# Up projections of three MLP quarters computed in the orientation of the down projections, a quarter of their products Strassen-like, with the results turned back by TensorE

## The chip, the cores and the metric

The kernel runs on one core of one Trainium2 chip. The metric is the device time of one execution in microseconds (us); for the kernel before it is 1199.64 us, the median of 3 runs (1199.57 to 1199.95).

## What is computed

One layer of a decoder over 256 tokens with 2048 channels: three kinds of attention and an output projection, a cross attention, and an MLP. The change touches the MLP alone:

```python
def rms_norm(x, g):
    y = x32 * lax.rsqrt(jnp.mean(x32 * x32, axis=-1, keepdims=True) + RMS_EPS)
    return (y * g.astype(jnp.float32)).astype(x.dtype)
...
h = rms_norm(x, g_mlp[l])
x = x + jnp.einsum('bsf,fd->bsd', jnp.square(jax.nn.relu(jnp.einsum('bsd,df->bsf', h, w_up[l]))), w_down[l])
```

`w_up` is 2048 x 8192 and `w_down` is 8192 x 2048, both float32.

## The kernel before

**Numbers.** Each float32 operand is split in a high part, rounded to the type fp32r, and a low part, the remainder. A product is three matmuls: high times high, high times low, low times high. ScalarE (ACT) makes the high half of a weight tile from `staged` into `w_high` (128x1024), VectorE (DVE) subtracts and writes `w_low`, and TensorE (PE) takes both. `w_high` and `w_low` hold four such halves; ACT may write half h when PE is done with half h-4 (semaphore `half_done`), DVE follows it (`high_ready`), PE follows DVE (`low_ready`). Weights come by DMAs of 1 MB on SyncE's queue into four slots of `staged`.

**The MLP.** The 8192 hidden channels are four quarters of 16 tiles of 128. For each quarter the up projection comes first, then the down projection.

- *Up* (L1539, `job_of` L1310, `half_job` L1282): one job for each of the 16 hidden tiles. The weight block is stationary, the 256 tokens are moving: for two blocks of the depth (`kt` even and odd) there are a 512-column matmul of the high weight with both parts of the tokens, two 256-column matmuls of the low weight, and another 512-column one. A job has 8 such pairs. Its output is laid channels by tokens; ACT and DVE make relu, the norm's factor (a row of `factor` by tokens), the square and the split, and put the tile into `part_b`.
- *Down* (`down_group` L1581): a quarter's outputs stay by tokens, 1024 channels in each of two groups. Here the activations are stationary (128 tokens), the weights moving with 512 columns. A quarter of the depth (the first unit of 4 blocks) is computed by seven products in place of eight, Strassen's scheme in the Winograd form: `s_half` (L1563) is one product, 6 matmuls, with sums of weight blocks that DVE makes in place (`sum_of_weights`, L1139) and sums of tokens (`sums_of_tokens`, L1102). The other three units are ordinary: four `r_half` (L1543) each, 12 matmuls in one. So a group has 7 x 6 + 12 x 12 = 186 matmuls of 512 columns. Halves in a group are numbered: 0 to 2 are three products, 3 to 6 the first ordinary unit, 7 to 10 the four products with sums (11 is counted together with 10), 12 to 19 the last two units. DVE adds the seven products and the four PSUM sums into `y` in 12 steps (`step`, L1158; semaphore `y_step`). The last four steps of a group stand in DVE's queue among the first halves of the group that follows.
- The fourth quarter's up and down projections are ordinary; between its up jobs PE turns `y` by two 128x128 transposes a job (L1632), so that DVE can add it to `x`.

**The start of the MLP.** The cross attention's output projection (`short_jobs`, JOB_CO) runs while ACT and DVE (`grow`, L625 and L1018) add its results to `x`, scale and split them into `part_a`, and split the first MLP weights. PE's first up job waits for `x2_low`, `low_ready` and `taken`. GpSimd (POOL) sums squares for the norm, which PE ends with `norm_sum` (L1352), and clears `y` (L411).

What sets the order of the work is each engine's queue, written out by hand, with the semaphores; nothing is scheduled by a tool.

## Time and profile before

| | |
|---|---|
| median of 3 runs | 1199.64 us (1199.57 to 1199.95) |
| the profiled execution, its own time | 1199.49 us |
| its span, first to last instruction | 1197.7 us |
| PE busy | 1181.8 us, 99% of the span |
| DVE busy | 853.0 us, 71% |
| ACT busy | 628.7 us, 52% |
| mean granted TensorE clock | 0.998 |

The profile's page gives, for one execution, how long each engine was busy; the trace behind it gives the start and the length of each instruction. A matmul is shown longer than it takes from PE's time, since matmuls overlap: the distance from one start to the next is what one costs. Times in the rows are us from the span's start, if not marked ns.

### The profile page before, as it was taken

Reading aid. Unit: us, or ns where it says so; the run is one execution under the profiler, and the core shown is the slowest. Engines: PE = TensorE matmul, PEld = TensorE weight load, DVE = VectorE, ACT = ScalarE, POOL = GpSimd, SP = SyncE. Lnnn points to the kernel's source line nnn. Section 1 sums busy time; section 2 is a strip of 40 time slices with the busy share of each in tenths; the row PEclk is TensorE's granted clock in tenths of the full one; section 3 lists DMA queues with packets and bytes.
Section 4 is the critical chain, followed back from the end, with each engine's and each line's share of the span. In section 5 each row is a group of like instructions: output and inputs, shape, how many; then the busy total and the mean of one; then the engine's idle time right before and its main releaser. Section 6 shows DMA issues by size and latency. Waiting matters only on the chain.

```text
span 1197.7 us, 19269 instructions
## 1 busy us (share of the span) xinstructions
PE 1181.8 (99%) x6776; PEld 1035.5 (86%) x6776; DVE 853.0 (71%) x1149; ACT 628.7 (52%) x927; POOL 177.6 (15%) x177
## 2 busy tenths in 40 slices
PE   9999999999999999999999999999999999999996
PEld 7888899999989989888888888888888888888885
DVE  5758766786667967676887666877767787666554
ACT  6445455554645657565544555544656454555442
POOL 2907400030322504300000000000000000000341
PEclk9999999999999999999999999999999999999999
DMA  9664543443644543455456454647454746555541
GB/s 361 251 256 170 205 176 140 149 167 140 231 161 171 186 166 141 145 207 202 175 178 252 176 178 172 211 150 271 175 177 140 274 156 221 189 177 187 199 140 70
DMA packets 51455, 224.43 MB, mean 187 GB/s; under 512 B 3792, under 2 KB 4176, under 8 KB 31696
## 3 DMA queue, kind: packets, MB, share of 16 engines
q1 hardware_dynamic: 50688, 220.22, 51.3%
q10 hardware_dynamic: 720, 3.59, 0.8%
q8 instruction: 30, 0.49, 0.2%
q14 instruction: 17, 0.14, 0.0%
HBM read 221.69 MB, written 2.10 MB: 187 GB/s over the span
## 4 chain that ended last, share of the span: by engine, by line
PE 94%; DVE 3%; ACT 1%; issue 1%; POOL 1%; DMA 1%; SPq 0%; DVEq 0%; ACTq 0%; POOLq 0%
PE bank L1303 16%; PE bank L1300 16%; PE bank L1301 15%; PE extra L1557 6%; PE extra L1559 5%; PE extra L1558 5%; PE bank L1305 4%; PE bank L1307 4%; PE bank L1306 4%; PE bank L1346 3%; PE bank L1348 3%; PE bank L1347 3%; DVE w_low L813 1%; PE bank L1570 1%; PE bank L1572 1%; PE bank L1571 1%
## 5 line engine op out<-in xcount | busy, mean ns | idle before, releaser
L813 DVE TENSOR_TENSOR w_low<-staged,w_high 128x1024 fp32r<-128x1024 f32 x311 | 390.1, 1269 | 145.3 <-ACT w_high L433 133.8
L433 ACT ACTIVATE w_high<-staged 128x1024 fp32r<-128x1024 f32 x304 | 314.5, 1053 | 188.9 <-PE bank L1303 80.4
L1301 PEld LDWEIGHTS bank<-part_a,w_low 128*128 128x128 f32 x1408 | 264.6, 188 | 61.3
L1300 PE MATMUL bank<-part_a,w_high 128*128 128x512 f32 x704 | 281.0, 399 | 1.2 <-DVE w_low L813 1.2
L1303 PE MATMUL bank<-part_a,w_high 128*128 128x512 f32 x704 | 278.5, 396 | 0.0
L1301 PE MATMUL bank<-part_a,w_low 128*128 128x256 f32 x1408 | 276.8, 278 | 0.0
L719 ACT ACTIVATE w_high<-staged 128x1024 fp32r<-128x1024 f32 x114 | 119.1, 1059 | 107.8 <-PE extra L1559 85.6
L1133 DVE TENSOR_TENSOR w_low<-staged,w_high 128x1024 fp32r<-128x1024 f32 x114 | 137.4, 1221 | 32.4 <-ACT w_high L719 31.0
L361 POOL TENSOR_TENSOR squares<-x 128x256 f32<-128x256 f32 (+1 forms) x31 | 36.2, 1168 | 681.8 <-DVE x L1257 658.2
L1300 PEld LDWEIGHTS bank<-part_a,w_high 128*128 128x128 f32 x704 | 133.7, 190 | 2.0 <-DVE w_low L813 1.2
L1303 PEld LDWEIGHTS bank<-part_a,w_high 128*128 128x128 f32 x704 | 131.9, 187 | 0.0
L1557 PE MATMUL extra<-w_high,part_b 128*128 128x512 f32 x288 | 112.7, 391 | 0.2
L1559 PE MATMUL extra<-w_high,part_b 128*128 128x512 f32 x288 | 112.1, 389 | 0.0
L1558 PE MATMUL extra<-w_low,part_b 128*128 128x512 f32 x288 | 112.1, 389 | 0.0
L1305 PE MATMUL bank<-part_a,w_high 128*128 128x256 f32 x384 | 110.1, 287 | 0.1
L1307 PE MATMUL bank<-part_a,w_low 128*128 128x256 f32 x384 | 108.7, 283 | 0.0
L1306 PE MATMUL bank<-part_a,w_high 128*128 128x256 f32 x384 | 108.6, 283 | 0.0
L1098 DVE TENSOR_TENSOR part_b<-hidden,part_b 128x256 f32 (+1 forms) x64 | 27.2, 426 | 71.6 <-ACT part_b L701 71.6
L1305 PEld LDWEIGHTS bank<-part_a,w_high 128*128 128x128 f32 x384 | 73.7, 192 | 0.5 <-POOL part_a L375 0.4
L1306 PEld LDWEIGHTS bank<-part_a,w_high 128*128 128x128 f32 x384 | 73.6, 192 | 0.1
L1307 PEld LDWEIGHTS bank<-part_a,w_low 128*128 128x128 f32 x384 | 73.6, 192 | 0.0
L699 ACT ACTIVATE hidden<-spare 128x256 f32<-128x256 f32 x64 | 26.7, 418 | 76.8 <-DVE spare L1094 76.8
(201 smaller groups left out, 1803.2 us busy)
## 6 DMA issues: line engine op xcount, KB each, us to landing
staged<-in_wup SPq DMA_DIRECT2D x64, 1024.0 KB, 4.8
staged<-in_wdown SPq DMA_DIRECT2D x64, 1024.0 KB, 5.1
staged<-in_wqk SPq DMA_DIRECT2D x32, 1024.0 KB, 4.8
staged<-in_wv SPq DMA_DIRECT2D x12, 1024.0 KB, 4.9
staged<-in_wbc SPq DMA_DIRECT2D x8, 1024.0 KB, 4.8
staged<-in_wmk SPq DMA_DIRECT2D x4, 1024.0 KB, 4.7
staged<-in_woa SPq DMA_DIRECT2D x4, 1024.0 KB, 4.7
staged<-in_wcq SPq DMA_DIRECT2D x4, 1024.0 KB, 4.9
```

The source lines that it names most:

```text
L433: nc.scalar.activation(w_high[:, job % 2, cols], staged[:, job % 4, cols], ACT.Copy).then_inc(high_ready, 1)
L813: tt(w_low[:, job % 2, cols], staged[:, job % 4, cols], f32(w_high[:, job % 2, cols]), ALU.subtract).then_inc(low_ready, 1)
L1133: tt(half_4d(w_low, h), src, f32(half_4d(w_high, h)), ALU.subtract).then_inc(low_ready, made)
L1300: mm(out[:, :], high, both, start=first, stop=False)
L1301: last = mm(out[:, 0:T], low, part[:, slot(kt), 0, :], start=False, stop=False)
L1303: last = mm(out[:, :], high, both, start=False, stop=last_tile)
L1305: mm(out[:, 0:T], high, part[:, slot(kt), 0, :], start=first, stop=False)
L1306: mm(out[:, 0:T], high, part[:, slot(kt), 1, :], start=False, stop=False)
L1307: last = mm(out[:, 0:T], low, part[:, slot(kt), 0, :], start=False, stop=last_tile)
L1557: mm(out[:, :], part_b[:, kt, 0, tokens], high, start=opens, stop=False)
L1558: mm(out[:, :], part_b[:, kt, 0, tokens], low, start=False, stop=False)
L1559: last = mm(out[:, :], part_b[:, kt, 1, tokens], high, start=False, stop=ends)
```

## The change

The three quarters whose down projection was by groups have their up projection by the same kind of groups. A quarter is now four groups of 20 halves, 0 and 1 up, 2 and 3 down, each 186 matmuls of 512 columns with the activations stationary (`part_a` for up, `part_b` for down). The weights are loaded by the same DMAs as in the down groups. What comes with it:

- The sums of tokens of the MLP's input (`part_x`) are made once, at the start, from four tiles that ACT scales again (`x2_gained`).
- An up group's sums are by tokens (`common`, four 128x512 pieces), gathered by 8 DVE steps (`up_step`). In the group that follows ACT makes relu with the norm's factor as a scale by partition (`relu`, 2 x 128x1024), squares it (`relu_square`, 2 x 128x1024), and PE turns it by 16 transposes of 128x128, in two batches of 8 (`hidden_turn`), into PSUM banks 2 and 3; ACT (`hidden_high`) and DVE (`hidden_lows`) split each batch into `part_b`. The first batch of group 1 is also copied to `quad`, from which DVE makes the sums of tokens.
- The first group of all has an order of its own (`PLACES`): its third product comes after the first ordinary unit.
- The products that used bank 3 use bank 0.
- `up` by jobs is left for the fourth quarter.

```diff
 SUMMED_QUARTERS = 3
 GROUP_HALVES = 20
-GROUP_STEPS = 12
-QUARTER_HALVES = 2 * QUARTER + 2 * GROUP_HALVES
+UP_STEPS, DOWN_STEPS = 8, 12
+QUARTER_STEPS = 2 * UP_STEPS + 2 * DOWN_STEPS
+QUARTER_HALVES = 4 * GROUP_HALVES
...
+PLACES = {False: (2, (3, 4, 5, 6)), True: (6, (2, 3, 4, 5))}
...
+            def relu(q, group, t):
+
+                act.wait_ge(y_step, group_steps(q, group) - 1 + t)
+                nc.scalar.activation(by_token[:, t, :], common[:, 2 * t:2 * t + 2, :].rearrange("p a c -> p (a c)"),
+                                     ACT.Relu, scale=factor[:, F_X2, T + t:T + t + 1]).then_inc(relu_made, 1)
+
+            def relu_square(q, group, t):
+                act.wait_ge(relu_made, turned_before(q, group) + t + 1)
+                nc.scalar.activation(by_token[:, t, :], by_token[:, t, :], ACT.Square).then_inc(square_made, 1)
+
+            def hidden_high(q, group, n):
+                tile = 8 * (group - 1) + 4 * n
+                act.wait_ge(group_turned, turned_before(q, group) + n + 1)
+                if tile == 0:
+                    nc.scalar.activation(quad[:, :, :], hidden_turned, ACT.Copy).then_inc(turned_moved, 1)
+                nc.scalar.activation(part_b[:, tile:tile + 4, 0, :], hidden_turned, ACT.Copy).then_inc(turned_high, 1)
...
+            def mlp_group(q, group, ahead=None):
+                turns = group in (1, 2)
+                if turns:
+                    relu(q, group, 0)
+                r_first(q, group, 1)
+                if turns:
+                    relu(q, group, 1)
+                r_first(q, group, 2)
+                if turns:
+                    for t in range(QT):
+                        relu_square(q, group, t)
+                move_common(q, group)
+                r_first(q, group, 3)
+                if turns:
+                    hidden_high(q, group, 0)
+                rest_of_group(q, group)
+                for n in range(4):
+                    (next_group if ahead is None else ahead)(q, group + 1, n)
...
+            grow(JOB_CO, OUT_CO, part_a, lambda t: t, G_MLP, x2_high, x2_low, first_ahead)
+            dve.wait_ge(taken, BANKS + OUT_MLP)
+            dve.sem_inc(y_step, FREE_STEPS)
+            dve.wait_ge(x2_scaled, 4)
+            sums_of_tokens(x2_gained, 0)
+            r_first(0, 0, 2, True)
+            sum_of_weights(0, 0, 0)
+            sums_low(part_x, x2s_high, 1, x2s_low)
+            r_first(0, 0, 3, True)
...
+            def hidden_turn(q, group, n):
+
+                for j in range(4):
+                    for t in range(QT):
+                        last = nc.tensor.transpose(hidden_turned[:, j, t * P:(t + 1) * P],
+                                                   by_token[:, t, (4 * n + j) * P:(4 * n + j + 1) * P], ident)
+                last.then_inc(group_turned, 1)
...
+                for n in range(4):
+                    r_half(q, group, 3 + n, n, 1, (0, 1))
+                    if turns and n == 1:
+                        pe.wait_ge(square_made, turned + 2)
+                        pe.wait_ge(turned_low, turned)
+                        hidden_turn(q, group, 0)
+                products(q, group, turns)
...
+            pe.wait_ge(y_step, FREE_STEPS - 4)
+            pe.wait_ge(x2_low, 4)
+            s_half(0, 0, 0, bank[0], block_of(0, 0, 0), ends=True)
+            s_half(0, 0, 1, extra[0], block_of(0, 1, 0))
...
+            norm_sum(N_X2, bank[3], cols=True)
```

Two places of the order. First PE, where the MLP starts: the last rows of the cross projection and the first of the MLP, before:

```order
L1306 MATMUL bank<-part_b,w_high 128x256
L1307 MATMUL bank<-part_b,w_low 128x256
L1300 MATMUL bank<-part_a,w_high 128x512 [waits x2_low,low_ready,taken]
L1301 MATMUL bank<-part_a,w_low 128x256 x2
L1303 MATMUL bank<-part_a,w_high 128x512
```

and with the change:

```order
L1410 MATMUL banks<-part_b,w_high 128x256
L1411 MATMUL banks<-part_b,w_low 128x256
L1671 MATMUL banks<-w_high,part_a 128x512 [waits low_ready,x2_low,y_step]
L1672 MATMUL banks<-w_low,part_a 128x512
L1673 MATMUL banks<-w_high,part_a 128x512
```

The first MLP matmul waits for `y_step` in place of `taken`. DVE counts `y_step` up after all its work of `grow`, which is the second place: DVE's queue at the end of `grow`, before:

```order
L1031 TENSOR_TENSOR x<-x,bank 128x256
L1023 SCALAR_TENSOR_TENSOR part_a<-x,gains,part_a 128x256 [waits x2_high] x4
L813 TENSOR_TENSOR w_low<-staged,w_high 128x1024 [waits high_ready]
L1230 UNCONDITIONAL_BRANCH [waits y_clear,factor_ready,taken]
L1230 ISA
L813 TENSOR_TENSOR w_low<-staged,w_high 128x1024 [waits high_ready]
```

and with the change:

```order
L1106 TENSOR_TENSOR x<-x,banks 128x256
L1098 SCALAR_TENSOR_TENSOR part_a<-x,gains,part_a 128x256 [waits x2_high] x4
L1205 TENSOR_TENSOR w_low<-staged,w_high 128x1024 [waits high_ready]
L1190 TENSOR_TENSOR token_sums<-by_token 128x2x128 [waits taken,x2_scaled]
L1191 TENSOR_TENSOR token_sums<-by_token 128x2x128
L1193 TENSOR_TENSOR token_sums<-token_sums,by_token 128x2x128 [waits token_made]
L1195 TENSOR_TENSOR token_sums<-by_token,token_sums 128x2x128 [waits token_made]
L1205 TENSOR_TENSOR w_low<-staged,w_high 128x1024 [waits high_ready]
L1219 TENSOR_TENSOR staged<-staged 128x2x4x128
L1199 TENSOR_TENSOR part_x<-token_sums,part_x 128x2x512 [waits x2s_high]
```

The counting up itself (a semaphore instruction) stands behind the third row there; the sums of the input's tokens and the first sum of weights come where the first up job's work stood.

Third, ACT in a group with turns (here group 1), from its second weight half of the first ordinary unit on, with the change:

```order
L766 ACTIVATE by_token<-common,factor 128x1024 [waits y_step]
L735 ISA
L731 REGISTER_ALU [waits landed1]
L732 ACTIVATE w_high<-staged 128x1024 [waits half_done]
L770 ISA
L771 ACTIVATE by_token<-by_token 128x1024 [waits relu_made]
L770 REGISTER_ALU
L771 ACTIVATE by_token<-by_token 128x1024 [waits relu_made]
L760 REGISTER_ALU [waits half_done]
L761 ACTIVATE common<-banks 128x512 [waits y_step]
L731 REGISTER_ALU
L732 ACTIVATE w_high<-staged 128x1024 [waits half_done]
```

ACT does relu, the next weight half and both squares ahead of the copy of `common` and the last weight half of the unit; before, nothing but the copy stood between weight halves there.

## Rows read from the trace of the kernel before

**Rows 1.** The page's first part: busy time, share of the span, instructions.
```profile
PE 1181.8 (99%) x6776; PEld 1035.5 (86%) x6776; DVE 853.0 (71%) x1149; ACT 628.7 (52%) x927; POOL 177.6 (15%) x177
```

**Rows 2.** Waits of PE from 450 us on: total us, times, longest.
```profile
PE bank L1300 <- DVE w_low L813: 1.2, 2, 0.9
```

**Rows 3.** Stretches: length, busy us (instructions) of PE, PEld, DVE, ACT, POOL; PEclk, DMA.
```profile
480.13:571.48 91.35, 90.19 (x516) 78.21 (x515) 62.65 (x95) 51.66 (x86) 8.27 (x6) 1.00 0.51 183
571.48:613.99 42.51, 42.48 (x188) 34.81 (x186) 34.71 (x37) 21.26 (x23) 0.00 (x0) 1.00 0.56 198
613.99:656.24 42.25, 42.25 (x187) 34.81 (x186) 34.65 (x35) 20.55 (x20) 0.00 (x0) 1.00 0.59 210
656.24:745.41 89.17, 89.17 (x514) 77.81 (x512) 60.59 (x89) 50.19 (x79) 0.00 (x0) 1.00 0.51 183
...
919.47:1004.35 84.88, 84.78 (x374) 69.56 (x372) 69.36 (x72) 41.82 (x43) 0.00 (x0) 1.00 0.57 202
```

**Rows 4.** PE in order of time, around transposes: start, length, line, operation.
```profile
427.85 0.60 PE L1510 MATMUL extra<-square,values 128*128 128x128 f32 x4
428.21 0.48 PE L1346 MATMUL bank<-w_high,part_b 128*128 128x512 f32 x1
428.52 0.39 PE L1347 MATMUL bank<-w_low,part_b 128*128 128x512 f32 x1
...
1009.91 0.38 PE L1632 MATMUL extra<-square,values 128*128 128x128 f32 x2
1010.05 0.48 PE L1300 MATMUL bank<-part_a,w_high 128*128 128x512 f32 x1
```

**Rows 5.** The stretch of the fourth quarter's 16 up jobs with their 32 transposes.
```profile
1004.35:1097.13 92.78, 92.78 (x546) 80.96 (x545) 63.19 (x94) 48.91 (x77) 0.00 (x0) 1.00 0.50 178
```

**Rows 6.** PE and DVE in order of time where the MLP starts.
```profile
480.13 0.40 PE L1300 MATMUL bank<-part_a,w_high 128*128 128x512 f32 x1
...
480.33 1.75 DVE L813 TENSOR_TENSOR w_low<-staged,w_high 128x1024 fp32r<-128x1024 f32 x1
...
482.68 1.66 DVE L1023 SCALAR_TENSOR_TENSOR part_a<-x,gains,part_a 128x256 fp32r<-128x256 f32 x4
484.35 1.23 DVE L813 TENSOR_TENSOR w_low<-staged,w_high 128x1024 fp32r<-128x1024 f32 x1
```

**Rows 7.** ACT and POOL there, in order of time.
```profile
484.22 0.71 ACT L646 ACTIVATE squares<-x 128x256 f32<-128x256 f32 x2
...
486.92 3.52 POOL L411 MEMSET values<- 128x4096 f32 x1
```

**Rows 8.** DVE and ACT in order of time at the start of the group of 613.99.
```profile
614.28 1.41 DVE L1176 TENSOR_TENSOR values<-values,extra 128x512 f32<-128x512 f32 x2 [0.49 <-PE extra L1559]
615.60 1.22 DVE L1148 TENSOR_TENSOR staged<-staged 128x1024 f32<-128x1024 f32 x1
616.74 1.22 DVE L1133 TENSOR_TENSOR w_low<-staged,w_high 128x1024 fp32r<-128x1024 f32 x1
...
614.19 1.06 ACT L719 ACTIVATE w_high<-staged 128x1024 fp32r<-128x1024 f32 x1 [1.66 <-PE extra L1559]
...
634.67 2.01 ACT L719 ACTIVATE w_high<-staged 128x1024 fp32r<-128x1024 f32 x2 [0.31 <-PE extra L1572]
```

**Rows 9.** PE at that group's half 3, in order of time.
```profile
618.07 0.46 PE L1557 MATMUL extra<-w_high,part_b 128*128 128x512 f32 x1
```

**Rows 10.** An ACT group by line from 460 us on: count, busy us, mean ns, idle before.
```profile
L699 ACT ACTIVATE hidden<-spare 128x256 f32<-128x256 f32 x64 | 26.7, 418 | 76.8 <-DVE spare L1094 76.8
```

**Rows 11.** The clock: PE's last row, and stretches as in rows 3.
```profile
1187.87 0.70 PE L1650 MATMUL extra<-squares,square 128*128 128x256 f32 x2 [0.99 <-ACT squares L798]
...
1192.60:1193.60 1.00, 0.00 (x0) 0.00 (x0) 1.00 (x2) 0.00 (x0) 0.00 (x0) 0.51 0.72 291
...
1.11:4.68 3.57, 3.57 (x8) 2.86 (x9) 0.00 (x0) 1.38 (x2) 0.23 (x1) 1.00 0.74 170
4.68:6.46 1.78, 1.78 (x9) 1.38 (x7) 0.61 (x2) 0.84 (x3) 0.00 (x0) 1.00 1.01 314
```

More of the change, by code:

```diff
@@ L307, in _, with load_unit @@
             stream(wco_in, JOB_CO, CROSS)
-            def load_up(q):
-                with sp.Fori(0, QUARTER // 4) as i:
-                    for s in range(4):
-                        load(wup_in[q * 16 + i * 4 + s, :, :], mlp(q, i), JOB_MLP + s)
-            def load_unit(q, g, unit, slot, free):
+            def load_unit(src, q, group, unit, slot, free):
                 for n in range(2):
@@ L623, in _, with grow, next_half @@
                     outputs_a(1)
-            def grow(job, n_out, norm, part, slot, gain, ready, free):
+            def grow(job, n_out, norm, part, slot, gain, ready, free, ahead=None):
+                def next_half(s, half):
+                    if ahead is not None and s >= 2:
+                        ahead(2 * (s - 2) + half)
+                    else:
+                        split(none, job + s + 2, half)
                 for s in range(4):
@@ L640, in grow @@
                         if late:
-                            split(none, job + s + 2, half)
+                            next_half(s, half)
                         for t in tiles:
@@ new lines, in first_ahead, with last_ahead @@
+            def first_ahead(n):
+                if n < 2:
+                    s_tile(0, 0, n, n)
+                else:
+                    r_first(0, 0, n - 2, True)
+            def last_ahead(q, group, n):
+                split(mlp(3), JOB_MLP + n // 2, n % 2)
+            grow(JOB_CO, OUT_CO, N_X2, part_a, lambda t: t, G_MLP, x2_high, 1, first_ahead)
+            for t in range(4):
+                nc.scalar.activation(x2_gained[:, t, :], x[:, t, :], ACT.Copy,
+                                     scale=gains[:, G_MLP + t:G_MLP + t + 1]).then_inc(x2_scaled, 1)
@@ L1035, in grow @@
                             lows((t, t + 1))
-                        split(none, job + s + 2, half)
+                        if ahead is not None and s >= 2:
+                            ahead(2 * (s - 2) + half)
+                        else:
+                            split(none, job + s + 2, half)
             dve.wait_ge(taken, BANKS + OUT_OA)
@@ new lines, in sums_of_tokens @@
+            def sums_of_tokens(src, made):
+                blocks = src.rearrange("p (a k) (m n) -> p a k m n", a=2, m=2)
+                first, second = ([blocks[:, :, k, m, :] for k in range(2)] for m in range(2))
+                to = [token_sums[:, :, n, :] for n in range(4)]
+                tt(to[0], second[0], second[1], ALU.add).then_inc(token_made, 1)
+                tt(to[2], first[0], second[0], ALU.subtract).then_inc(token_made, 1)
+                dve.wait_ge(token_made, made + 1)
+                tt(to[1], to[0], first[0], ALU.subtract).then_inc(token_made, 1)
+                dve.wait_ge(token_made, made + 3)
+                tt(to[3], first[1], to[1], ALU.subtract).then_inc(token_made, 1)
@@ new lines, in up_step @@
+            def up_step(q, group, n):
+                c11, c12, c21, c22 = (common[:, k, :] for k in range(4))
+                to, one, two = ((c12, c11, bank[2]), (c21, c12, bank[0]), (c22, c21, bank[1]), (c12, c12, bank[1]),
+                                (c11, c11, extra[0][:, :]), (c21, c21, extra[2][:, :]),
+                                (c12, c12, extra[1][:, :]), (c22, c22, extra[3][:, :]))[n]
+                wait_for_step(q, group, n, {0: H_SUMS + 3, 4: H_C + 2, 6: H_C + 4})
+                tt(to, one, two, ALU.add).then_inc(y_step, 1)
@@ new lines, in _ @@
+            right_below(0, 0, PLACES[True][0], False)
+            products(0, 0, False)
+            pe.wait_ge(x2_low, KT)
+            for n in range(4):
+                r_half(0, 0, H_B + n, n, 2, ())
+            norm_sum(N_X2, bank[3], cols=True)
+            for n in range(4):
+                r_half(0, 0, H_C + n, n, 3, ())
+            with pe.Fori(0, SUMMED_QUARTERS - 1) as q:
+                for group in range(1, 5):
+                    mlp_group(q, group)
+            for group in range(1, 4):
+                mlp_group(SUMMED_QUARTERS - 1, group)
```

552 lines of the change are left out of this document (283 added, 269 removed).

## The prediction, made before the changed kernel ran

> **What bounds the kernel.** First the page's engine shares: PE is busy for 99% of the span, DVE for 71%, ACT for 52% [rows 1]. A busy PE proves little, since matmuls are shown overlapping, so next PE's waits: over the whole MLP two waits of 1.2 us in all, both in the first up jobs [rows 2]. Then the stages: an up quarter is 89.17 us, a quarter's two down groups 84.88, the later group of the first pair 42.25 [rows 3]. In all of them PE goes from matmul to matmul. So the time of the MLP is PE's columns and instructions, plus any hand-off that now comes late. The sum goes over the stretch from 480.13 (first up matmul) to 1004.35 (first up matmul of the fourth quarter); what follows is the same code in both kernels, and what comes before is too. In the kernel before, this stretch is 524.22 us.
>
> **Term 1, the up quarters become groups.** Out go 91.35 us and twice 89.17. In come six groups of 186 matmuls. A down group is the same instructions with another stationary operand, so it is priced by 42.25: 42.25 / 186 = 0.2272 us a matmul. All twelve groups make 507.0 us. Taken against the groups that were there (42.51 + 42.25 + 2 x 84.88 = 254.5), the new six cost 252.5 and replace 269.7. I take 42.25, not 42.51, because the 0.26 more of the first group comes from DVE, which arrives there from an up quarter with work left over; in the new kernel every group but one follows a group.
>
> **Term 2, the transposes.** 2 batches of 8 for each of 2 up groups a quarter: 96 in all. Four transposes take 427.85 to 428.21, and the matmul behind them takes 0.31 where 0.23 is normal [rows 4]: 0.44, or 0.11 each. The fourth quarter has 32 between its jobs and is 92.78 - 89.17 = 3.61 us longer [rows 3, 5], 0.113 each. A batch of 8: 0.88 to 0.90; twelve of them: **10.7 us**. The low end is the pace inside a pair, 0.14 us from its start to the next matmul [rows 4], or 0.07 each with 0.08 once for a batch: 0.64, in all 7.7.
>
> **Term 3, the start.** PE is done with the cross projection at 480.13 and went straight on. Now its first matmul also waits for `y_step`, which DVE counts up only behind the last split of `grow`. DVE's queue there is a split of 1.75 from 480.33, two additions, four low parts from 482.68, and another split from 484.35 [rows 6]. No row shows whether a semaphore instruction goes while the operation before it runs. I take it that it does, since it needs nothing of the split, and PE starts at about 484.5; the late end is the split's own, 485.6. The new gap is **4.4 us** (to 5.5). In exchange what the old first quarter had over a plain one goes (91.35 is taken out whole, 2.2 above 89.17: two waits of 1.2 in all [rows 2] and the norm's sum). The new first group then has room: ACT ends its squares at 484.93 [rows 7] and makes four scaled tiles by 486.7; DVE needs 1.5 us for four additions, then split (1.14), sum, low sums, split. Half 4 is ready at 489.4 and wanted at 484.5 + 2 x 1.36 + 2 x 2.73 = 492.7; half 5 at 492.8, wanted 495.4; half 7, four more DVE passes later, at 498.5, wanted 499.5. Nothing late. The norm's sum with its two new column matmuls: **0.7**, an estimate, since 2.2 less 1.2 leaves 1.0 for the sum and the restarts of PE after its waits.
> At this place row and rule can be weighed. A DVE pass with both inputs in SBUF took 1.75 and not 1.23 while POOL was adding [rows 6]; POOL's clearing of `y` (3.52 us from 486.92 [rows 7]) ran while DVE had nothing to do, so no row tells whether it holds DVE. If it did, the first group's chain would come 3.7 us later and the sum grow by 2.8. The Trainium skill, page "SBUF — State Buffer", section "SBUF: two separate sides", says that a DVE operation with two SBUF inputs contends only with a GpSimd operation that reads SBUF; a clearing reads nothing, and by that rule the sum stays.
>
> **Term 4, inside a group with turns** (times from its first matmul). PE reaches the turn at 18 + 24 matmuls = 9.5. ACT: half 3 ends at 1.26 [rows 8]; relu, half 4, relu, half 5 and two squares, six passes at 0.96, the second of two back to back (2.01 less 1.06 [rows 8]), end at 7.0; the copy of `common` and half 6 at 8.5. PE does not wait. The turn ends at 10.4. In group 1 ACT now copies twice (to 12.7), DVE subtracts (14.0, a 128x1024 pass from PSUM taken as 1.14, the distance in rows 8; as two 128x512 steps it would be 1.41 [rows 8]), makes half 7 (15.1; wanted 15.9), half 8 (16.3), the four sums of tokens (17.8) and half 9 (19.0, seen by PE 19.15). Half 9 is wanted at 15.9 + 2.73 = 18.6: late by 0.54, three times: **1.6 us**. In group 2 a copy and the sums are missing, so nothing is late. The second batch comes between ordinary halves of 2.73 us each; the low parts are ready 1.5 to 2 us before the last unit wants them. The extra DVE and ACT work of an up group is hidden by its 42.25 us (a down group leaves DVE 7.6 and ACT 21.7 us free [rows 3], and an up group has 8 steps where down has 12).
> At each group's edge the chain is tight already: DVE's two last steps, a sum of weights and half 3 start at 614.28, 615.60 and 616.74 [rows 8] and PE takes half 3 at 618.07, its first matmul there shown 0.46 long [rows 9]. It has no slack and no loss. An up group's last steps are of the same shape, so I add nothing. DMAs: the same 1 MB loads, asked for at the same halves as in a down group, where PE waited for none.
>
> **Sum.** 4.4 + 507.0 + 10.7 + 1.6 + 0.7 = 524.4 against 524.2: +0.2 us. The profiled execution took 1199.49 with a span of 1197.7, so I predict 1199.7; the median of the runs, 1199.64, lies 0.15 above that execution, and I leave this aside. A measurement of this kernel can tell a change of about 0.2%, 2.4 us: below 1197.2 is faster, above 1202.0 slower.
>
> **The rivals.**
> *The clock falls in the gap.* PE stood for 4.06 us after its last matmul and then the granted clock was 0.51, the level of 1.2 GHz [rows 11]; the new gap is 4.4 us. At the program's start eight matmuls took 3.57 us where nine later took 1.78 [rows 11]: about 1.8 us lost before the clock is back. 1201.5. For it: the gap's length; against: the fall is seen once, after a sparse stretch. The Trainium skill, page "TensorE: Matmul & The Clock Gate", Part 1, has idle stretches throw PE back to 1.2 GHz and calls the moment run-variable; the trace agrees with the fall.
> *Each group costs what the first did*, 42.51: DVE's tight edge slips because the up groups add a little to its chain. 12 x 0.26 = 3.1: 1202.8.
> *ACT's chain comes late* (the slower side): relu, squares and copies run at four times the 256-wide rate, 0.418 [rows 10], 1.67 a pass. The point is 1.55 us: four passes, two halves at 0.96 and 1.26 must end by 9.4. At 1.67 the turn waits 0.5 us, six times, and group 1's two copies bring half 9 later by 1.4, three times: +7.2, 1206.9. Against: one 128x1024 pass took 1.06 [rows 8].
> *Clearing `y` blocks DVE*: 1202.5, as above.
> *The transposes run at the pair's inner pace*: -3.0, 1196.7. Against: both longer rows say 0.11.
> *The change does not do what it says*: the seven products save 6 of 192 matmuls a group, 1.36 us; that much is counted in the instructions, and only the up stage's price could differ with `part_a` stationary. The rows give no sign of it.
>
> **How the numbers follow.** My sum: 0.50, with most of it within 0.2%. Clock: 0.12, its price just below the bound, a half of it slower. Group edge 0.12, ACT late 0.08, clearing 0.05, all slower. Transposes cheaper 0.13, faster. Of my sum I give 0.02 to faster and 0.03 to slower for hand-offs mis-sized. Faster 0.15, same 0.51, slower 0.34. The range leaves out ACT's case and the tails: 1196.5, just under the cheap transposes, to 1204.0, which takes in the late end of the start (+1.1) with any one of the three other slower rivals.
>
> **What would show it.** Right: PE's first MLP matmul near 484.5, groups of 42.25 us, those with two turns 44.0, group 1 about 44.6, transposes x8 with 0.9 to the next matmul's end, and the fourth quarter starting near 1004.5. Wrong: PE waits on ACT's `by_token` (ACT late), a PEclk under 1.00 near 485 (clock), or a group period off by more than 0.2 us.

## The result: slower by 0.25%, and the profile after

| | before | after |
|---|---|---|
| median, 13 runs each on one chip | 1199.56 us (1199.27 to 1200.30) | 1202.44 us (1201.54 to 1204.56) |
| the profiled execution, its own time | 1199.49 us | 1202.02 us |
| its span | 1197.7 us | 1200.2 us |
| mean granted clock | 0.998 | 0.995 |

The ratio is 1.0025, with a 95% interval of 1.0016 to 1.0033: slower, by a little more than what the prediction called measurable. The time lies inside the predicted range, 2.7 us above the predicted 1199.7; by the prediction's own bound of 1202.0 it is slower, which had 0.34, and not the same, which had 0.51. The first part of the page, which answers to [rows 1]:

```profile
PE 1181.2 (98%) x6456; PEld 1022.5 (85%) x6456; DVE 888.3 (74%) x1097; ACT 639.6 (53%) x848; POOL 177.3 (15%) x177
```

PE has 320 instructions fewer and is busy 0.6 us less, while the span is 2.5 us longer. So look at where PE stood. PE's waits from 450 to 1010 us (total, times, longest) answer to [rows 2]; the second row lies in the cross attention, ahead of the MLP, and before has such a wait of 0.8 us too:

```profile
PE banks L1671 <- DVEq L1335: 4.2, 1, 4.2
PE banks L1636 <- DVE qk L1151: 0.8, 1, 0.8
```

One wait in the MLP, at its first matmul, on DVE's sequencer: on the counting up of `y_step`. Then the stages, to be held against [rows 3, 5]: columns as there. The first row is the gap, the second the first group; then groups 1, 2 (with turns), 3, 4 (without), 5, 6 (with), 7; last the fourth quarter's up jobs.

```profile
480.86:485.17 4.31, 0.16 (x3) 0.00 (x1) 4.30 (x9) 2.39 (x5) 2.40 (x3) 1.00 0.00 0
485.17:530.09 44.92, 44.92 (x193) 36.92 (x194) 33.71 (x34) 23.30 (x28) 5.90 (x4) 0.96 0.53 187
530.09:574.40 44.31, 44.27 (x204) 36.46 (x202) 36.72 (x38) 27.74 (x28) 0.00 (x0) 1.00 0.54 190
574.40:618.50 44.10, 44.10 (x204) 36.47 (x202) 36.83 (x37) 25.77 (x26) 0.00 (x0) 1.00 0.56 191
618.50:660.74 42.24, 42.24 (x188) 34.82 (x186) 34.66 (x35) 20.43 (x20) 0.00 (x0) 1.00 0.58 199
660.74:703.00 42.26, 42.26 (x188) 34.65 (x186) 32.07 (x31) 20.44 (x20) 0.00 (x0) 1.00 0.58 200
703.00:747.49 44.49, 44.45 (x204) 36.59 (x204) 36.72 (x38) 27.75 (x28) 0.00 (x0) 1.00 0.55 190
...
1006.85:1099.63 92.78, 92.78 (x546) 81.00 (x545) 62.92 (x94) 48.91 (x77) 0.00 (x0) 1.00 0.50 177
```

Groups without turns take 42.24 and 42.26, as the down groups did before, groups with turns 44.05 to 44.49, and the fourth quarter's 92.78 is the 92.78 of [rows 5]. What doesn't fit is in the first two rows: PEclk 0.96 in the first group, and a start at 480.86 where before it was 480.13. PE in order of time at the MLP's start (start, length, line, operation, idle before and its releaser), against [rows 6]:

```profile
485.17 0.50 PE L1671 MATMUL banks<-w_high,part_a 128*128 128x512 f32 x1 [4.15 <-DVEq L1335]
485.50 0.40 PE L1672 MATMUL banks<-w_low,part_a 128*128 128x512 f32 x1
...
486.24 0.63 PE L1672 MATMUL banks<-w_low,part_a 128*128 128x512 f32 x1
486.66 0.63 PE L1673 MATMUL banks<-w_high,part_a 128*128 128x512 f32 x1
...
489.61 0.39 PE L1659 MATMUL extra<-w_high,part_a 128*128 128x512 f32 x1
```

and the stretch in which the granted clock was at 1.2 GHz, by its row:

```profile
486.15:489.56 3.41, 3.41 (x9) 2.65 (x9) 2.39 (x6) 2.58 (x5) 3.33 (x3) 0.50 0.00 0
```

After the gap of 4.31 us PE ran for 1.0 us at full speed, then eight matmuls stood 0.43 us apart in place of 0.23. The twelve matmuls of the first two products took 489.61 - 485.17 = 4.44 us. The clock fell, as the first rival had it (e1 will show what they take without the fall). DVE and POOL at the same place:

```profile
485.08 1.23 DVE L1205 TENSOR_TENSOR w_low<-staged,w_high 128x1024 fp32r<-128x1024 f32 x1
487.29 0.70 DVE L1190 TENSOR_TENSOR token_sums<-by_token 128x256 f32<-128x256 f32 x1 [0.98 <-ACT by_token L836]
487.91 0.41 DVE L1191 TENSOR_TENSOR token_sums<-by_token 128x256 f32<-128x256 f32 x1
...
489.04 1.22 DVE L1205 TENSOR_TENSOR w_low<-staged,w_high 128x1024 fp32r<-128x1024 f32 x1
```
```profile
485.50 2.21 POOL L388 TENSOR_TENSOR acc<-acc,quad 128x256 f32<-128x256 f32 x2 [2.08 <-ACT quad L670]
487.65 3.52 POOL L429 MEMSET values<- 128x4096 f32 x1
```

DVE's split starts at 485.08. The counting up of `y_step` stands behind it in DVE's queue, and still PE starts at 485.17: the semaphore went while the split ran, not at its end. And DVE's passes under the clearing of `y` take their usual 0.41 and 1.22, while the one under POOL's additions took 0.70.

Inside group 1, the turn on PE and the late half 9:

```profile
539.38 0.39 PE L1661 MATMUL extra<-w_high,part_a 128*128 128x512 f32 x1
539.61 1.03 PE L1688 MATMUL banks<-square,by_token 128*128 128x128 f32 x8
540.40 0.47 PE L1659 MATMUL extra<-w_high,part_a 128*128 128x512 f32 x1
540.71 0.39 PE L1660 MATMUL extra<-w_low,part_a 128*128 128x512 f32 x1
...
548.46 0.39 PE L1673 MATMUL banks<-w_high,part_x 128*128 128x512 f32 x1
548.89 0.50 PE L1671 MATMUL banks<-w_high,part_x 128*128 128x512 f32 x1
```

A batch: 0.79 us and 0.08 in the matmul behind it, 0.87. Half 9: 0.43 us from start to start, so 0.2 late; the matmul behind the wait took another 0.34 in place of 0.23 (548.89 to 549.23), so that the wait costs PE 0.3 in all.

**A sum that a noisy start leaves alone.** From here on I compare kernels by the stretch from the end of the cross projection to the fourth quarter's first matmul: before 480.13 to 1004.35, **524.22 us**; after 480.86 to 1006.85, **525.99 us**. What follows it takes the same time in both. So the profiled execution's +2.5 us are +1.8 in the stretch and +0.7 in the part ahead of it, whose instructions the change leaves as they were.

### The profile page after: what moved, and what is told of

It is laid out like the page before. It is cut to its first block, busy times and chain, and to the rows that moved or that the text cites. A ratio compares the mean times of both kernels' runs of the same rounds, so it can differ in the third digit from the quotient of the medians.

```text
span 1200.2 us, 18023 instructions
## 1 busy us (share of the span) xinstructions
PE 1181.2 (98%) x6456; PEld 1022.5 (85%) x6456; DVE 888.3 (74%) x1097; ACT 639.6 (53%) x848; POOL 177.3 (15%) x177
## 4 chain that ended last, share of the span: by engine, by line
PE 92%; DVE 3%; DMA 2%; ACT 1%; issue 1%; POOL 0%; SPq 0%; DVEq 0%; ACTq 0%
PE extra L1659 11%; PE extra L1661 11%; PE extra L1660 11%; PE banks L1407 8%; PE banks L1404 8%; PE banks L1405 8%; PE banks L1409 4%; PE banks L1411 4%; PE banks L1410 4%; PE banks L1450 2%; PE banks L1452 2%; PE banks L1451 2%; DMA staged<-in_wv 2%; PE banks L1671 2%; PE banks L1673 2%; PE banks L1672 2%
## 5 line engine op out<-in xcount | busy, mean ns | idle before, releaser
L888 DVE TENSOR_TENSOR w_low<-staged,w_high 128x1024 fp32r<-128x1024 f32 x215 | 275.2, 1289 | 117.5 <-ACT w_high L451 110.6
L1205 DVE TENSOR_TENSOR w_low<-staged,w_high 128x1024 fp32r<-128x1024 f32 x228 | 276.3, 1226 | 78.8 <-ACT w_high L732 77.6
L1405 PEld LDWEIGHTS banks<-part_a,w_low 128*128 128x128 f32 x640 | 120.4, 188 | 27.3
L379 POOL TENSOR_TENSOR quad<-x 128x256 f32<-128x256 f32 (+1 forms) x31 | 37.0, 1195 | 656.4 <-DVE x L1361 631.8
L1404 PE MATMUL banks<-part_a,w_high 128*128 128x512 f32 x320 | 129.0, 403 | 0.0
L1407 PE MATMUL banks<-part_a,w_high 128*128 128x512 f32 x320 | 126.7, 396 | 0.0
L1405 PE MATMUL banks<-part_a,w_low 128*128 128x256 f32 x640 | 126.0, 278 | 0.0
L1659 PE MATMUL extra<-w_high,part_a 128*128 128x512 f32 x288 | 113.1, 393 | 0.0
L1661 PE MATMUL extra<-w_high,part_a 128*128 128x512 f32 x288 | 112.3, 390 | 0.0
L1660 PE MATMUL extra<-w_low,part_a 128*128 128x512 f32 x288 | 112.2, 390 | 0.0
L1409 PE MATMUL banks<-part_a,w_high 128*128 128x256 f32 x384 | 110.3, 287 | 0.1
L1411 PE MATMUL banks<-part_a,w_low 128*128 128x256 f32 x384 | 108.8, 283 | 0.0
L1410 PE MATMUL banks<-part_a,w_high 128*128 128x256 f32 x384 | 108.8, 283 | 0.0
L1409 PEld LDWEIGHTS banks<-part_a,w_high 128*128 128x128 f32 x384 | 73.7, 192 | 0.5 <-POOL part_a L393 0.4
L1410 PEld LDWEIGHTS banks<-part_a,w_high 128*128 128x128 f32 x384 | 73.7, 192 | 0.1
L1411 PEld LDWEIGHTS banks<-part_a,w_low 128*128 128x128 f32 x384 | 73.7, 192 | 0.0
L1659 PEld LDWEIGHTS extra<-w_high,part_b 128*128 128x128 f32 x288 | 54.1, 188 | 12.6 <-DVE w_low L1205 1.0
```

The lines of the kernel that those rows point to most:

```text
L888: tt(w_low[:, job % 2, cols], staged[:, job % 4, cols], f32(w_high[:, job % 2, cols]), ALU.subtract).then_inc(low_ready, 1)
L1205: tt(half_4d(w_low, h), src, f32(half_4d(w_high, h)), ALU.subtract).then_inc(low_ready, made)
L1404: mm(out[:, :], high, both, start=first, stop=False)
L1405: last = mm(out[:, 0:T], low, part[:, slot(kt), 0, :], start=False, stop=False)
L1407: last = mm(out[:, :], high, both, start=False, stop=last_tile)
L1409: mm(out[:, 0:T], high, part[:, slot(kt), 0, :], start=first, stop=False)
```

## The experiments

Theory A is that the changed kernel's time is 1199.7 plus what the trace shows: about 1.6 us of slow clock in the first group. Each kernel stands here with its own profiled execution and median, and each ratio is to before measured beside it, whose median was 1199.56 to 1199.66. After was measured once, not again beside the experiments.

| kernel | MLP reached at | stretch | median (range), runs | ratio to before [95%] |
|---|---|---|---|---|
| before | 480.13 | 524.22 | 1199.56 (1199.27 to 1200.30), 13 | |
| after | 480.86 | 525.99 | 1202.44 (1201.54 to 1204.56), 13 | 1.0025 [1.0016, 1.0033] |
| e1 keep busy | 480.97 | 524.57 | 1200.82 (1200.12 to 1202.54), 10 | 1.0012 [1.0003, 1.0022] |
| e2 early start | 481.82 | 524.00 | 1201.00 (1199.74 to 1202.71), 10 | 1.0011 [1.0001, 1.0020] |
| e3 half the transposes | 481.03 | 521.67 | 1198.89 (1197.09 to 1200.43), 10 | 0.9992 [0.9982, 1.0001] |
| b1 gap in before | 479.65 | 528.97 | 1204.09 (1203.75 to 1204.87), 5 | 1.0039 [1.0025, 1.0053] |
| e4 sums later | 481.08 | 525.34 | 1201.29 (1200.54 to 1203.23), 11 | 1.0012 [1.0003, 1.0021] |
| e5 both | 480.84 | 524.82 | 1202.00 (1200.34 to 1204.38), 11 | 1.0021 [1.0012, 1.0030] |
| b2 memory layout | 480.08 | 524.26 | 1199.55 (1199.18 to 1199.77), 11 | 0.9998 [0.9989, 1.0007] |
| b3 PE written out | 480.21 | 524.21 | 1199.66 (1199.28 to 1200.52), 11 | 1.0000 [0.9991, 1.0009] |
| b4 declarations | 480.00 | 524.20 | 1199.51 (1199.12 to 1199.98), 11 | 0.9999 [0.9990, 1.0008] |
| b5 all written out | 480.61 | 524.22 | 1199.88 (1199.59 to 1200.59), 11 | 1.0003 [0.9994, 1.0012] |
| **e6 new start** | 480.90 | 522.08 | **1197.97** (1197.31 to 1199.12), 11 | 0.9986 [0.9977, 0.9995] |
| e7 e6 without the jump | 480.60 | 522.45 | 1198.55 (1198.16 to 1200.21), 11 | 0.9995 [0.9986, 1.0004] |

### e1: PE kept busy in the gap

```diff
-            pe.wait_ge(y_step, FREE_STEPS - 4)
             pe.wait_ge(x2_low, 4)
+            busy = part_a[:, 0, :, :].rearrange("p a n -> p (a n)")
+            for n in range(18):
+                mm(extra[3][:, :], part_a[:, 0, 0, 0:P], busy, start=True, stop=True)
+            pe.wait_ge(y_step, FREE_STEPS - 4)
```

Nothing reads the 18 products.

> Eighteen extra 512-column matmuls fill the gap at the start of the MLP (their result is not used); nothing else changes. 18 x 0.227 is 4.1 us, under the gap of 4.31. Theory A (the gap lets the clock fall, and the fall costs 1.7 us by itself): the granted clock stays at 1.00 through the start, the first MLP matmul still starts near 485, the time is 1.7 us less than the changed kernel, about 1200.7, and the spread of its runs shrinks from 3 us to about 1. Rival B (the low clock is harmless, since DVE sets the pace of the first group anyway): the same 1202.4.

PE in order of time in e1:

```profile
480.97 4.27 PE L1745 MATMUL extra<-part_a 128*128 128x512 f32 x18
485.31 0.50 PE L1671 MATMUL banks<-w_high,part_a 128*128 128x512 f32 x1
...
488.21 0.39 PE L1659 MATMUL extra<-w_high,part_a 128*128 128x512 f32 x1
```

The first MLP matmul starts 4.34 us after the cross projection, as late as in after (4.31), but the twelve matmuls take 488.21 - 485.31 = 2.90 us and not 4.44: 1.54 us less with work that nobody needs. The stretch is 1.42 shorter, the median 1.62, as Theory A had it. That settles the clock's share in the profiled executions. The spread is a miss: 2.4 us where about 1 was expected. The two slowest of the ten runs (1202.33 and 1202.54) have a mean clock of 0.996, the others 0.997 or 0.998, so the clock may fall a second time in some runs, at a place that no profile here shows.

### b1: the same gap put into the kernel before

DVE counts `x2_grown` up behind `grow` (its wait for `taken` moves ahead of that), and PE's first up job waits for it.

```diff
+            dve.sem_inc(x2_grown, 1)
...
+            pe.wait_ge(x2_grown, 1)
             for s in range(4):
```

> The kernel before, with one more wait: PE's first up job waits until DVE is at the end of its work on the input, as in the changed kernel. Theory A: a gap of 4.3 us, in which the clock falls; PE's two old waits of 1.5 us from start to start go, the fall costs 1.7: plus 4.5 us, 1204.1. Rival B (the fall came from something else of the change): plus 2.8, 1202.4, the clock at 1.00.

```profile
479.53 0.28 PE L1309 MATMUL bank<-part_b,w_low 128*128 128x256 f32 x1
483.93 0.73 PE L1302 MATMUL bank<-part_a,w_high 128*128 128x512 f32 x1 [4.12 <-DVEq L1228]
484.46 0.63 PE L1303 MATMUL bank<-part_a,w_low 128*128 128x256 f32 x2
```
```profile
484.03:487.44 3.41, 3.41 (x11) 2.93 (x12) 1.04 (x1) 0.39 (x2) 3.10 (x3) 0.50 0.30 72
```

The wait without the rest of the change costs the kernel before 4.4 us in the median and 4.75 in the stretch, near the expected 4.5: the gap and the slow clock behind it, less a part of its two old waits. So in the changed kernel the start is a debt of about 5.9 us (4.31 and 1.54), and the groups pay all but 1.8 of it back.

### e3: half of the transposes left out

```diff
-                for j in range(4):
+                for j in range(0, 4, 2):
```

PE turns four of the eight pieces of a batch; half of the hidden activations are not computed.

> Each batch turns every second hidden tile only: 4 transposes in place of 8, so half of the transposes are left out and the hidden values of those tiles are stale. Theory A (a transpose costs 0.11 us wherever it stands, here 0.79 to 0.87 a batch): 48 less, 4.8 to 5.3 us less, 1197.1 to 1197.6, less what DVE's lateness at half 9 of group 1 takes back (PE arrives there 0.4 earlier, three times: 1.2), so 1198.3 to 1198.8. Rival B (a batch has a fixed price, by switching to transposes and back): under 2 us less.

```profile
539.79 0.60 PE L1688 MATMUL banks<-square,by_token 128*128 128x128 f32 x4
540.14 0.48 PE L1659 MATMUL extra<-w_high,part_a 128*128 128x512 f32 x1
...
701.31 0.39 PE L1661 MATMUL extra<-w_high,part_a 128*128 128x512 f32 x1
702.18 0.49 PE L1671 MATMUL banks<-w_high,part_a 128*128 128x512 f32 x1 [0.48 <-issue]
```

Groups with turns are 0.80 to 0.88 us shorter, 5.0 in all for 48 transposes: 0.105 each, as costed. The stretch is only 4.3 shorter, because PE stands for 0.6 us at 702, where it jumps back to the start of its loop over quarters and no engine held it up (its releaser is "issue"). The median, 1198.89, is near the expected 1198.3 to 1198.8, but partly by luck: half 9 was expected to take 1.2 us back, and stands 0.44 from start to start (548.20, 548.64), as in after; the stop at 702 came in its place.

### e2: PE starts without `y_step`

```diff
-            pe.wait_ge(y_step, FREE_STEPS - 4)
+            pe.wait_ge(taken, BANKS + OUT_CO + 13)
             pe.wait_ge(x2_low, 4)
...
             right_below(0, 0, PLACES[True][0], False)
+            pe.wait_ge(y_step, FREE_STEPS - 4)
             products(0, 0, False)
```

> PE's first MLP matmul waits for the addition that empties its bank, and no longer for the end of DVE's work on the input. Theory A (the wait on the last split's place in the queue makes the gap): PE goes on at once, no fall of the clock, but DVE is then late for halves 4, 5 and 7 by about 1.25, 0.7 and 1.65 us, so only 2.4 of the 6.0 us come back: about 1200.1. Rival B (DVE's chain alone sets the first group's end): no gain beyond the clock's 1.7 us, 1200.7. Rival C (nothing else binds): 1196.4.

PE's waits in e2, as above:

```profile
PE banks L1671 <- DVE w_low L1205: 1.4, 1, 1.4
PE extra L1659 <- DVE w_low L1205: 1.4, 2, 1.0
```

The gap is gone (481.70 to 481.82) and the clock stays at 1.00, yet of 4.3 us of gap and 1.5 of clock the stretch gives only 2.0. PE now waits for the halves of the first group, 1.35, 0.79 and 1.83 us from start to start (490.06, 494.03, 498.79), where Theory A had them late by 1.25, 0.7 and 1.65: DVE, in this order of its work, doesn't supply them sooner. In after, the wait at the start had given DVE that time. The median, 1201.00, is above both 1200.1 and Rival B's 1200.7, since this kernel's profiled execution reaches the MLP 1.7 us late; the stretch's 2.0 lies between A's 2.4 and B's 1.7. Three of its ten runs (1201.48 to 1202.71) have a mean clock of 0.996, so the clock did not stay up in all of them.

### e4: group 1's sums of tokens after half 12

The four sums on DVE go behind the first half of the last but one unit (half 12), and their high part on ACT behind its third (half 14). DVE's part of the edit:

```diff
-                if group == 1:
-                    sums_of_tokens(quad[:, :, :], q * 4 + 4)
                 s_sum(q, group, 2)
                 s_sum(q, group, 3)
                 r_tile(q, group, H_B, SLOT_RB[g], 0)
+                if group == 1:
+                    sums_of_tokens(quad[:, :, :], q * 4 + 4)
```

> In group 1 of each quarter DVE makes the sums of tokens behind the weight halves 7 to 12, in place of between 8 and 9, and ACT their high parts behind half 14. Theory A (DVE reaches half 9 of group 1 late by 0.43 us from start to start less 0.23 for the matmul itself, 0.2 us, three times): 0.6 us less, 1201.8. Rival B (the group's extra 0.5 us beyond 42.25 and two batches has another cause): the same 1202.4.

```profile
548.60 0.39 PE L1673 MATMUL banks<-w_high,part_x 128*128 128x512 f32 x1
548.82 0.39 PE L1671 MATMUL banks<-w_high,part_x 128*128 128x512 f32 x1
```

Half 9 is no longer late, and Rival B is out: the three groups 1 take 44.01, 44.14 and 44.19 us, where they took 44.31, 44.49 and 44.40, so 0.86 less in all, 0.3 each and not the 0.2 that the expectation counted. The stretch is 0.65 shorter, since the jump ahead of the second quarter cost more in this execution. The median is 1.15 lower, more than that; the ranges of the two kernels overlap widely, and I take the stretch's number.

### e5 and e6: both, and a new order in the first group

e5 has the edits of e2 and e4, and DVE's sums of the first group changed so that each sum of weights comes right ahead of its low pass.

```diff
-            sum_of_weights(0, 0, 2)
-            sum_of_weights(0, 0, 3)
-            rest_of_group(0, 0, next_group)
+            s_sum(0, 0, 0)
+            s_sum(0, 0, 1)
+            for n in (2, 3):
+                sum_of_weights(0, 0, n)
+                s_sum(0, 0, n)
+            rest_of_group(0, 0, next_group, False)
```

> The early start, the later sums of tokens, and in the first group DVE makes the low parts of halves 7 and 8 ahead of the last two sums of weights. Theory A: 1201.0 of the early start alone, less 1.6 for the wait at half 7, plus up to 0.8 where half 10 is now late, less 0.6: 1199.6. Rival B (DVE's chain in the first group is only shuffled): 1200.4 or more.

The longest wait on PE, and DVE and ACT in order of time ahead of it:

```profile
505.37 0.50 PE L1672 MATMUL extra<-w_high,part_a 128*128 128x512 f32 x1 [1.95 <-DVE w_low L1205]
```
```profile
501.63 1.22 DVE L1219 TENSOR_TENSOR staged<-staged 128x1024 f32<-128x1024 f32 x1
504.09 2.36 DVE L1205 TENSOR_TENSOR w_low<-staged,w_high 128x1024 fp32r<-128x1024 f32 x2 [1.24 <-ACT w_high L732]
```
```profile
502.93 2.95 ACT L732 ACTIVATE w_high<-staged 128x1024 fp32r<-128x1024 f32 x3 [2.48 <-DVE staged L1219]
```

A miss: 1202.00 where 1199.6 was expected. DVE sums, ACT waits 2.5 us for the sum and makes its high half, DVE waits 1.2 us for that and makes the low one: the two engines take turns instead of overlapping, and PE stood 2.3 us. In 8 of the 11 runs the mean clock was 0.994 to 0.996 (times 1201.82 to 1204.38), in the others 0.997 and 0.998 (1200.34 to 1201.45): with such a gap the clock probably falls in most executions, though in the profiled one it did not.

e6 keeps the two edits and puts one piece of DVE's work between each sum and its low pass, with the four scaled tiles made one weight half sooner on ACT.

```diff
             s_sum(0, 0, 0)
+            sum_of_weights(0, 0, 2)
             s_sum(0, 0, 1)
-            for n in (2, 3):
-                sum_of_weights(0, 0, n)
-                s_sum(0, 0, n)
+            sum_of_weights(0, 0, 3)
+            s_sum(0, 0, 2)
+            s_sum(0, 0, 3)
```

> The early start of e2 and the later sums of e4 together (as in e5), with DVE's order in the first group changed again: first product's weights, a sum of weights, second product's weights, a sum of weights, so that ACT's high pass of one half runs while DVE makes the sum for the next; ACT makes the four scaled tiles one weight half earlier. Theory A (what the changed kernel loses at the start is the gap with its slow clock, and in e5 the serial chain of sum, high pass, low pass): PE starts the MLP near 481.8 and waits under 1 us in all in the first group; against e2's 1201.0 this is -2.0 for its stalls and -0.6 for the three half 9s: 1198.4. Rival B (the first group's supply is bound by DVE and ACT whatever the order): waits of 2 us or more remain, 1200.4 or later. Rival C (the kernels of the changed family carry about +1.2 us from the program's first 31 us): then the MLP's own stretch shrinks as A says, but the time stays above 1199.5.

Its waits, and its stretch as a row:

```profile
PE extra L1665 <- DVE w_low L1209: 0.9, 2, 0.5
PE banks L1677 <- DVE w_low L1209: 0.6, 1, 0.6
```
```profile
480.90:1002.98 522.08, 520.52 (x2337) 427.99 (x2335) 427.12 (x434) 287.49 (x294) 7.70 (x7) 1.00 0.56 194
```

1197.97 us: 1.6 below before, 4.5 below after, and the interval leaves 1 out, narrowly. Rival C (above 1199.5) is out. The waits sum to 1.5 us where I expected under 1, but the stretch is 1.9 below e2's. So the change does pay, about 2.1 us of the MLP's 524, when its start is arranged for it. The gain is small beside what these runs can tell: e7, the same work without a jump, is 1.1 below before with 1 inside its interval. And before's own start was not arranged: its two waits cost PE 1.5 us from start to start, and how much of that an order made for it would give back was not tested.

### What shifts the part ahead of the MLP: b2, b3, b4, b5, e7

All kernels of the changed family reach the MLP 0.5 to 1.7 us late, and their runs spread over 1.8 to 4.0 us, where before's spread over 0.8 to 1.4 in four of its five series (in the fifth, of 33 runs, one at 1201.85 makes it 2.6). One profiled execution can be off by as much itself: b1, whose code ahead of the MLP is before's, got there 0.5 us early. In the profiled executions the delay arises in the first 31 us, while the first weights load. Before and after from 5 to 10 us, columns as above (the last is GB/s):

```profile
5.00:10.00 5.00, 4.55 (x20) 3.27 (x18) 2.82 (x6) 3.47 (x7) 0.00 (x0) 1.00 1.02 375
```
```profile
5.00:10.00 5.00, 4.66 (x20) 3.31 (x18) 2.90 (x6) 3.38 (x6) 0.00 (x0) 1.00 0.97 324
```

The queues that carry instructions move 0.63 MB before (0.49 and 0.14) and 0.86 MB after (0.70 and 0.16), by the page. Four runs ask what that has to do with it, and a fifth asks about a jump. b2 gives the kernel before the changed kernel's memory layout; b4 adds its single PSUM tensor and nine more semaphores; b3 writes out PE's loops over the first three quarters' up jobs and over the quarters, b5 those on SyncE, ACT and DVE as well:

```diff
-            with pe.Fori(1, SUMMED_QUARTERS) as q:
-                with pe.Fori(0, QUARTER // 4) as i:
+            for q in range(1, SUMMED_QUARTERS):
+                for i in range(QUARTER // 4):
```

> The kernel before with the changed kernel's memory layout: rope in the region that hidden later overlays, spare and squares in one tensor, by_token, part_x and the larger common allocated; the work is the same. In the profiled executions the changed kernels reach the MLP 0.7 to 1.7 us later than the kernel before, and the delay arises in the first 31 us, while the first weights land. Theory L (the layout slows the first transfers): plus 1.2 us, 1200.8. Rival P (it is the larger program, or chance of the profiled executions): 1199.6.

> The kernel before with PE's loops over the quarters and their up jobs written out (4559 rows for PE where 3413 were; the changed kernel has 3891): the same work, a larger program. Theory P (a larger program makes the start, or the fetching of instructions, slower): 1 us or more above 1199.6. Rival L (the layout): 1199.6.

> The kernel before, computing the same with the same instructions; its memory is declared as the changed kernel declares it (the tensors of the changed layout, PSUM as one tensor of four banks, nine more semaphores that nothing uses). Theory D (the +0.7 to +1.2 us by which the changed kernels reach the MLP late comes from what is declared): the MLP starts 0.7 us or more later than 480.1, its runs spread by 2 us or more, median 1200.3 to 1200.8. Theory A (it does not): 1199.6, spread under 1.3 us, MLP at 480.1.

> The kernel before with the MLP's loops over its down groups written out on PE, ACT, DVE and SP alike, so that all four engines' programs are longer; the instructions that run are the same. Theory E (the late start of the changed kernels comes from longer programs on several engines at once, whose loading shares the DMA engines with the first weights): the MLP starts 0.7 us or more later than 480.1, spread 2 us or more, median 1200.3 to 1200.8. Theory A: 1199.6, spread under 1.3 us, MLP at 480.1.

b2, b3 and b4 change nothing that shows: 1199.55, 1199.66, 1199.51, MLP at 480.08, 480.21, 480.00 (the intervals of the three ratios would still allow 0.8 to 1.1 us). b5 moves it a little: 480.61, 1199.88. In its 5 to 10 us the DMAs moved no more than after's:

```profile
5.00:10.00 5.00, 4.41 (x20) 3.34 (x19) 2.76 (x6) 3.63 (x6) 0.00 (x0) 1.00 1.00 311
```

But b3 was as slow there (309 GB/s) and lost 0.1 us. In the profiled executions the kernels with longer programs (b3, b5 and the changed ones) moved 299 to 324 GB/s in 5 to 10 us, those with before's program (before, b1, b2, b4) 359 to 375. That goes with the length, but not by Theory E's way: in the first 31 us the queues that carry instructions moved 0.02 MB in before, b3, b5 and after alike. It may explain a part of the shift (0.3 us in b5's median, with 0.87 MB of instructions, as many as after's); the interval of b5's ratio holds 1, so not even that is certain.

e7 takes the other hint, PE's stop at the jump in e3: it is e6 with that loop written out.

> e6 with PE's loop over the quarters written out: the same instructions run, but PE does not jump back to the start of its four groups when the second quarter begins (in e3 PE stood from 701.31 to 702.18 there, 0.5 us of it put down to issue; in the changed kernel the first matmul behind the jump takes 0.31 in place of 0.23, in e4 and e5 there are 0.36). Theory J (this jump, short in the profiled executions, is long in others and makes the wide spread of the changed kernels' runs): no matmul distance over 0.25 us at the quarter's start, the spread falls from e6's 1.8 us to 1.2 or less, and the median lies 0.2 to 0.8 below e6's 1197.97. Theory K (the spread comes from the program's first 31 us, which this leaves alone, or makes worse through PE's longer program): median 1197.9 to 1198.5, spread 1.5 us or more.

Theory J fell: at 699.47, where the second quarter starts, no distance is over 0.25 us, but the range is 2.05 us wide, and the median is 0.6 higher than e6's, as Theory K had it. The jump is not what spreads the runs.

## Why the prediction was right, and where it was not

**Term 1, the groups: right.** 42.24 to 42.28 us in the five groups without turns; rows of the down groups priced up groups to 0.1%. The rivals "each group costs what the first did" and "the change does not do what it says" are out.

**Term 2, the transposes: right.** 0.87 a batch, 10.4 in all against 10.7; e3 has 0.105 for one. The cheap rival (0.64) is out.

**Term 3, the start: right in its gap, not in what followed it.** The gap was 4.31 against 4.4, and the choice behind it (a semaphore instruction goes while the operation ahead of it in the queue runs) is what the rows show. The norm's sum cost about 0.87 (518.30 to 519.09, and 0.08 behind it) against 0.7. The clearing of `y` held up nothing; the rule that I weighed there, from the Trainium skill, page "SBUF — State Buffer", section "SBUF: two separate sides", agrees with the passes of 0.41 and 1.22 us under the clearing.

**The step that failed** is the weight on the clock: 0.12 for "the clock falls in the gap", with 1.8 us. It fell in the profiled executions of after, e3, e4 and b1, each with a gap of 4.28 to 4.31 us, and cost 1.54 us. In the profiled executions of e1, where the gap was filled, and of e2, e5, e6 and e7, with distances of at most 2.3 us, it stayed. I had rows with a stand of 4.06 us and the clock at 0.51 behind it [rows 11], and called that a sparse stretch; the row nearest to a case should have carried it. The price that I gave it, 1.8 us, was 0.3 too high (and not what its row says: eight matmuls at the later pace, nine in 1.78, would take 1.6 us, so the row has a loss of 2.0). With the measured price the sum is 1201.2, still under the bound of 1202.0: the clock alone doesn't make the result. The Trainium skill, page "TensorE: Matmul & The Clock Gate", Part 1, has idle stretches throw PE back to the lower clock, and these four falls agree.

**Term 4: the mechanism right, its size not.** Half 9 came late in each group 1, by 0.2 us (0.3 with the slower matmul behind it) and not by 0.54: DVE started on the low parts at 12.65 us of the group as predicted, but its passes follow each other at 1.14, and half 9 was seen at 18.8 and not 19.15. ACT did relu and both squares by 537.3, 7.2 us into the group (7.0 predicted); "ACT late" is out.

**In no term and no rival:** the +0.7 us ahead of the MLP (1.1 in the medians: 2.9 less the stretch's 1.8). I wrote that what comes before the stretch is the same code, and left it at that. It is the same code in a different program, and that was not free here. Its cause stays open: memory layout, declarations and PE's length moved nothing singly, and the length of all programs together gives at most a part. In e6 the slowest run (1199.12) has a mean clock of 0.995, and in e7 two of the three slowest (1199.68 and 1200.21) have 0.995 and 0.996, against 0.997 and 0.998 in the others. That could be one more fall of the clock; no such run was profiled, so where it would fall is not known.

The balance of the profiled execution: 1199.7 predicted, +1.54 clock, +0.73 ahead of the MLP, +0.2 norm, -0.3 transposes, -1.0 for half 9, -0.1 gap, comes to 1200.8. Of the 1.3 us to the measured 1202.02, 0.3 is the slower matmul behind each half 9. The rest lies in small pieces that I don't place: 0.26 in the first group, 0.6 over the six groups with turns. Two errors of 0.7 us offset each other, which is luck: half 9 was priced that much too high, and the part ahead of the MLP stood in no term.

## What to carry to other kernels

When a stage gets cheaper but its first instruction needs more operands ready, price the start of the stage apart: here a wait of 4.3 us and the clock behind it cost 5.9 us, and a saving spread over 520 us had to pay for it. Start PE on what is ready, and order the feeding engines so that a sum, its high part on one engine and its low part on the other overlap with other work; e6 turned +2.9 into -1.6 us by order and waits alone. Compare stretches between two events inside the kernel beside whole times, since a shift ahead of the stage can be as large as the effect.

## What the runs showed of the hardware

- The clock fell about when PE resumed, not early in the gap: 1.0 us behind the first matmul in after (485.17, 486.15), 0.1 behind it in b1 (483.93, 484.03), 0.1 ahead of it in e4 (485.39, 485.27). The first matmuls behind a gap can be at full speed, as in after, and a look at them alone misses the loss.
- Useless matmuls held the clock in e1's profiled execution, and its 18 made the kernel 1.6 us faster in the median.
- A fp32 transpose of 128x128 costs 0.10 us in a batch of 8 (0.79 us) and 0.09 in one of 4 (0.35 us), from the first start to the start of the next matmul, which then takes 0.08 longer.
- In two places of after where a pass of DVE and an addition of POOL overlap, both reading SBUF, the one that started first kept its usual time. DVE's split at 485.08 took its usual 1.23 us though POOL's addition is shown from 485.50, and that addition took 1.40 where the one behind it took 0.73; DVE's pass at 487.29, started while POOL added, took 0.70 in place of 0.41. In before, the split of 1.75 us started while POOL added, and the next one (484.35), ahead of POOL's addition at 484.76, took 1.23: it was not POOL's adding alone that made a pass long, as the prediction read it.
- DVE counted `y_step` up behind a split of 1.23 us that had started at 485.08, and PE was released at 485.17: the count does not wait for the end of the operation ahead of it.
